# A state-space scan on one Trainium2 core: group loop unrolled, the next group's projection placed inside the scan, convolution read from PSUM, low weight parts on VectorE

## What is computed

```python
xbc = jax.nn.silu(causal_dwconv(xbc, conv_w, conv_b))      # xbc = hn @ w_in[...], 3072 columns, 4 taps
xs, Bm, Cm = split_cols(xbc, (SSD_D_INNER, SSD_BC, SSD_BC))
def ssd_chunk_step(S, inp):                                # 4 groups, 8 heads of 64, chunks of 64, state 128
    xdt, a, Bc, Cc = inp
    acum = jnp.cumsum(a, axis=1)
    seg = jnp.exp(-jnp.abs(acum[:, :, None] - acum[:, None, :]))
    cb = jnp.einsum('btgn,bsgn->btsg', Cc, Bc)
    y = jnp.einsum('btsgr,btsg,bsgrp->btgrp', seg, cb, xdt)
    y = y + jnp.einsum('btgn,bgrpn,btgr->btgrp', Cc, S, jnp.exp(acum))
    to_end = jnp.exp(acum[:, -1:] - acum)
    S = S * jnp.exp(acum[:, -1])[..., None, None] + jnp.einsum('bsgn,bsgr,bsgrp->bgrpn', Bc, to_end, xdt)
    return S, y
y = y + d_skip * xs_h
```

## Time and profile before

| | |
|---|---|
| runs | 2955.06, 2955.79 and 2959.34 us, median 2955.79 us |
| span of the profiled execution | 2945.8 us; its own time is not given apart, the runs lie 9.3 to 13.5 us above the span |
| busy over the span | PE 2838.9 us (96%), DVE 1991.9 (68%), ACT 1002.5 (34%), POOL 626.4 (21%) |
| `ssd_phase` | from 51.3 to 358.5 us, that is 307.2 us |

### The profile page before, as it was taken

The page is one execution under the profiler, slowest core; times in us unless marked ns, Lnnn a source line. Parts: engine busy times, 40 slices in busy tenths (PEclk is TensorE's granted clock), DMA queues, the critical chain, the costliest instruction groups (busy, mean ns, idle before and its releaser), DMA issues. The chain is left out here.

```text
span 2945.8 us, 43610 instructions
## 1 busy us (share of the span) xinstructions
PE 2838.9 (96%) x16114; PEld 2517.0 (85%) x16114; DVE 1991.9 (68%) x3329; ACT 1002.5 (34%) x1494; POOL 626.4 (21%) x444
## 2 busy tenths in 40 slices
PE   6999999999999999999999999999999999999998
PEld 5777677799787899999999999999999776788877
DVE  5878755334635468989967768777777655478843
ACT  3222244233333234344433333333334333322222
POOL 2333200000000037555654322222221000100000
PEclk9999999999999999999999999999999999999999
DMA  2111122211122237688999989999996211222232
GB/s 94 40 39 43 43 93 93 86 58 57 64 93 100 93 123 270 218 281 284 288 290 330 386 310 342 342 341 342 342 341 238 64 51 43 71 89 99 92 87 79
DMA packets 273015, 496.38 MB, mean 169 GB/s; under 512 B 121313, under 2 KB 178785, under 8 KB 272114
## 3 DMA queue, kind: packets, MB, share of 16 engines
q1 hardware_dynamic: 217586, 335.20, 34.4%
q0 software_dynamic: 36864, 134.23, 12.4%
q10 hardware_dynamic: 18432, 25.17, 2.3%
HBM read 442.10 MB, written 52.43 MB: 168 GB/s over the span
## 5 line engine op out<-in xcount | busy, mean ns | idle before, releaser
L283 PE MATMUL banks<-experts_third,weights_high 128*128 128x384 f32 x1024 | 346.1, 338 | 1.0 <-DVE experts_third L2024 1.0
L285 PE MATMUL banks<-experts_third,weights_low 128*128 128x384 f32 x1024 | 346.0, 338 | 0.0
L284 PE MATMUL banks<-experts_third,weights_high 128*128 128x384 f32 x1024 | 346.0, 338 | 0.0
L283 PE MATMUL banks<-hn_high,weights_high 128*128 128x264 f32 (+1 forms) x832 | 280.2, 337 | 7.8 <-PEq L515 2.9
L284 PE MATMUL banks<-hn_low,weights_high 128*128 128x264 f32 (+1 forms) x832 | 273.7, 329 | 0.0
L285 PE MATMUL banks<-hn_high,weights_low 128*128 128x264 f32 (+1 forms) x832 | 273.6, 329 | 0.0
L1838 POOL TENSOR_TENSOR weights_low<-weights_raw,weights_high 128x1024 fp32r<-128x1024 f32 x63 | 151.3, 2402 | 489.7 <-ACT weights_high L1740 489.5
L1797 ACT ACTIVATE weights_high<-weights_raw 128x1024 fp32r<-128x1024 f32 x128 | 135.9, 1062 | 346.7 <-PE banks L285 346.7
L283 PE MATMUL banks<-hb_high,weights_high 128*128 128x384 f32 x688 | 242.3, 352 | 9.5 <-POOL weights_low L1838 5.2
L284 PE MATMUL banks<-hb_low,weights_high 128*128 128x384 f32 x688 | 235.3, 342 | 0.0
L285 PE MATMUL banks<-hb_high,weights_low 128*128 128x384 f32 x688 | 235.2, 342 | 0.0
(11 more groups left out here) (565 smaller groups left out, 7125.3 us busy)
## 6 DMA issues: line engine op xcount, KB each, us to landing
weights_raw<-in_u SPq DMA_DIRECT2D x128, 512.0 KB, 6.9
weights_raw<-in_v SPq DMA_DIRECT2D x128, 512.0 KB, 5.8
early_experts<-experts_A ACTq DMA_DIRECT2D x128, 192.0 KB, 4.6
expert_weights<-shared SPq DMA_DIRECT2D x48, 512.0 KB, 7.4
shared<-expert_weights SPq DMA_DIRECT2D x128, 192.0 KB, 5.5
shared<-early_experts SPq DMA_DIRECT2D x128, 192.0 KB, 6.3
weights_raw<-in_w_up SPq DMA_DIRECT2D x44, 512.0 KB, 3.2
weights_raw<-in_w_xbc SPq DMA_DIRECT2D x24, 512.0 KB, 3.2
```

The costliest lines, as they stand in the source:

```text
L283: nc.tensor.matmul(to, w[0], x[0], start=start, stop=False)
L284: nc.tensor.matmul(to, w[0], x[1], start=False, stop=False)
L285: return nc.tensor.matmul(to, w[1], x[0], start=False, stop=stop)
```

## The change

`ssd_phase` is rewritten, and nothing else. Its parts:

1. The loops over groups are unrolled on every engine; semaphores are compared with constants.
2. The group's 6 tiles of the projection are moved: those of group 0 run first as before, those of group g + 1 are put between the steps of the scan of group g. The scan of the last group has `keep_running` in those places (14 matmuls in all); in the other groups there are none.
3. The product is convolved from PSUM. ScalarE's eviction (Copy) becomes the first tap and the bias (Identity with scale and bias, `first_tap`); the other three taps are three scalar_tensor_tensor of VectorE with the PSUM pair as one input, over all 528 positions, into a buffer that is shifted by an offset. The tensor_scalar goes.
4. The weight split: the high part moves from VectorE to ScalarE (`weight_high`), the low part from GpSimd to VectorE, behind each convolution (`split_low`).
5. The scaling by the skip weight moves from GpSimd to ScalarE. GpSimd keeps the 20 diagonals. Abs and Exp work on 4 blocks at once, one set a group.
6. PSUM: the projection has one pair of banks (0, 1; tile 1 of each group uses 4, 5) once the scan runs, where it had three; row part, turn-back, within and before have one bank each, where they had two. A tile's product waits for the last tile's convolution.

The core of the diff (the order on TensorE, and the two helpers that moved):

```diff
-                    for j in range(T):
-                        pe.wait_ge(low_done, g * T + j + 4)
...
-                        for b in SIDE.get(j, ()):
-                            row_part(b)
+                for m in range(T):
+                    tile_product(m)
+                    if m < 5:
+                        row_part(0, m)
+                for g in range(G):
+                    m, ahead = (g + 1) * T, g + 1 < G
+                    turn_x(g, 0)
+                    turn_x(g, 1)
+                    if ahead:
+                        tile_product(m)
+                    else:
+                        keep_running(k, 0, 3)
+                    if g:
+                        turn_back(g - 1, NB - 1)
+                    turn_x(g, 2)
+                    products_inside(g)
+                    turn_b(g)
+                    if ahead:
+                        tile_product(m + 1)
...
+                    turn_x(g, 3)
+                    turn_x(g, 4)
+                    if ahead:
+                        tile_product(m + 2)
...
+                    state_part(g, 0)
+                    state_part(g, 1)
+                    within(g, NB)
+                    within(g, 0)
+                    state_part(g, 2)
+                    before(g, 0)
+                    state_part(g, 3)
+                    if ahead:
+                        row_part(g + 1, 0)
+                        tile_product(m + 3)
+                    turn_back(g, NB)
+                    within(g, 1)
+                    before(g, 1)
+                    state_part(g, 4)
+                    state_part(g, 5)
+                    turn_back(g, 0)
+                    if ahead:
+                        row_part(g + 1, 1)
+                        tile_product(m + 4)
...
+                def weight_high(m):
...
+                    act.wait_ge(product, m - 1)
+                    nc.scalar.activation(high[:, m % 2, :], raw_w[:, m % 3, :], ACT.Copy).then_inc(high_done, 1)
...
+                def split_low(m):
+
+                    dve.wait_ge(high_done, m - 1)
+                    nc.vector.tensor_tensor(low_w[:, m % 2, :], raw_w[:, m % 3, :], high[:, m % 2, :].bitcast(F32), ALU.subtract
+                                            ).then_inc(low_done, 1)
+
+                def convolve(m):
+                    g, j = m // T, m % T
+                    dve.wait_ge(tap, m + 1)
+                    for s in (1, 2, 3):
+                        if m or s > 1:
+                            dve.wait_ge(convolved, 3 * m + s - 1)
+                        to = acc_at(m, s).rearrange(two, h=2)
+                        nc.vector.scalar_tensor_tensor(to, B[:, pair(m):pair(m) + 2, 0:264], conv[:, g, j, 3 - s:4 - s], to,
+                                                       ALU.mult, ALU.add).then_inc(convolved, 1)
+                    split_low(m + 2)
```

More of the change, by code:

```diff
@@ L989, in ssd_phase @@
         diag64 = k.const("diag64")
+        two = "p (h n) -> p h n"
+        full, meta = slice(0, P), slice(0, META)
         def heads(a, n=HD):
@@ new lines, in row_part @@
+                def row_part(g, b):
+                    r, n = rows_of(b)
+                    pe.wait_ge(diag, g * 5 + b + 1)
+                    if g or b:
+                        pe.wait_ge(diff, g * 5 + b)
+                    if g and b == 0:
+                        pe.wait_ge(m_ready, g * 5)
+                    nc.tensor.matmul(B[r, ROW_BANK, 0:H * n], k.const("same")[r, r] if b < NB else k.const("ones")[r, r],
+                                     X[r, b % 2, 0:H * n], start=True, stop=True).then_inc(row_done, 1)
@@ new lines, in before, with turn_back @@
+                def before(g, b):
+                    pe.wait_ge(state, g * 8 + 2 + 2 * b)
+                    for i in range(2):
+                        c = 1 + 2 * b + i
+                        last = nc.tensor.matmul(B[i * CH:i * CH + CH, BEFORE, :], bc[:, g % 2, 1, chunk_cols(c)],
+                                                S[:, (c - 1) % 4, :], start=True, stop=True)
+                    last.then_inc(y_done, 1)
+                def turn_back(g, b):
+                    r = full if b < NB else meta
+                    pe.wait_ge(y_tok, g * 5 + place(b))
+                    if g or b < NB:
+                        pe.wait_ge(y_out, g * 5 + place(b) - 1)
+                    for j in range(4):
+                        n = P if b < NB else META
+                        last = nc.tensor.transpose(B[:, BACK_BANK, j * n:(j + 1) * n], yt[r, 1 if b == NB else b % 2, j * P:(j + 1) * P],
+                                                   ident[r, r])
+                    last.then_inc(y_turned, 1)
@@ L1291 @@
+                add_skip(G - 1, NB - 1)
 SCORE_STEPS = 5 * (2 * PEER_HEADS + PEER_HEADS) + 25
```

553 lines of the change are left out of this document (303 added, 250 removed).

## The result

The changed kernel takes **2930.48 us** (median of 4 runs, 2928.13 to 2936.58) against 2955.43 (4 runs, 2950.99 to 2959.34): ratio 0.9925, 95% interval 0.9906 to 0.9943. It is faster by 0.75%, some 22 us by the ratio where 38 were forecast; the sign is as predicted. The median is 12 us over the forecast of 2918 and inside the range of 2903 to 2932, at its upper end. By the ratio, taken from the 2955.8 that the forecast started from, the time is 2933.6 us, just above that range. A third of the expected gain and more is missing, and the question is where it went.

A forecast was written before the change was run, and what follows sets the result against it. TensorE bounds a new group (58.7 us of work against VectorE's 51); 91.4 + 59.8 + 61.9 + 61.9 + 42.6 = 317.6 us against 358.5, less 3 for handovers, saves 38: 2918 us, range 2903 to 2932.

The forecast's parts named there:

- the mechanism of the overlap: In ssd_phase neither TensorE nor VectorE is full over a 77 us group, so projection and scan can be overlaid.
- The last scan: Group 3's scan, with no tiles left to overlay: 5.9 to the first turn, 34.3, and two bank waits, together 42.6 us.
- two waits of 1.2 for banks that aren't doubled any more: In the last scan, 1.2 us lost twice because banks are single; 2.4 us in the sum.
- The 5.9 to the first turn: Start of the last scan: 5.9 us until TensorE first turns x.
- TensorE's work per group: In each new group, tiles, turns, state products, within, before and row parts add up to 58.7 us.
- The waits (1.2 and 2.0 a group): Groups 1 and 2: TensorE waits 1.2 us for block 0's skip and 2.0 for the small row part's difference.
- The clock in overlapped groups: TensorE's granted clock was expected at 1.00 in the three overlapped groups; below 0.95 would show the forecast wrong.
- Rival 5: TensorE falls to 1.2 GHz in groups without dummies, up to 3022 us with all 18 tiles slow; chance 0.03.
- VectorE: 51 us of work in a new group, taps from PSUM at 0.74 us each, under TensorE's 58.7.
- GpSimd: Keeps only diagonals; taps with one SBUF input run free of it, low parts on VectorE can be held up.
- Rival 3, the lists interlock: TensorE and VectorE wait for each other on single banks, 1.5 us at four places a group; 2938 us, chance 0.08.
- The reading of the baseline: Runs of the kernel before were taken to lie about 10 us above the profiled span, left as it is.

The follow-up runs named there:

- the same kernel without the rotation: Changed kernel, but each group's six projection tiles stand ahead of its own scan again; 2997.32 us, ratio 1.0152 to the kernel before.
- The old order: Changed kernel with the last scan, from the third state on, in the previous kernel's step order, doubled banks, two more fillers: 2916.89 us; on the reordered kernel 2907.44.
- the reordered kernel: Changed kernel with VectorE's difference for row part 3 ahead of tile 5's low part, and meta rows turned back ahead of tile 3; 2917.76 us, ratio 0.9894.
- three kernels with more fillers: Filler matmuls added in group 0 and the last scan: to the changed kernel 2931.0 us, with doubled banks 2936.61, with doubled banks on the reordered kernel 2931.33.

## Why the prediction was right or wrong

- **Direction and the mechanism of the overlap: right.** Neither engine was full over a group, and laying the stages over one another paid: 67 us against the same kernel without the rotation.
- **The last scan: the step that failed.** The term was "what the scan of before has behind its convolutions, 38.2 less 3.9 = 34.3, and two waits of 1.2 for banks that aren't doubled any more: 42.6". It measured 54.3. The 5.9 to the first turn was right (289.98 to 295.95). The rest took durations from a scan whose order of steps, and whose clock, are others: the order rows showed where the tiles went, and I compared no others. The 11.7 us over the forecast are, by the stretches of the table:
  - 3.1 ahead of the first state (18.9, where the forecast had 13.8 and 2.0 more). VectorE has 3.7 us more of work there than in the scan of before (15.45 us busy against 11.73): the low part for the next phase, two skips, two differences and the tokens of the last block, less the first tap that ScalarE now makes. Low parts on GpSimd took 1.0 to 1.1 off this stretch (17.8 and 17.9 us). For the exponentials, which begin only behind the last difference, VectorE waits 0.15 us.
  - 6.0 in the middle. The parts within of the meta rows and of block 0 stand ahead of the third state, which costs about 6 at half clock and about 2 at full clock.
  - 3.9 to the end. A turn-back that waits for VectorE stands ahead of block 2, worth about 2; the rest goes with the clock (0.83).
  - 1.1 between the cut at 358.5 and the start of the next phase, less 2.4 for the single banks, which were charged for nothing: doubling them alone gave nothing.

  The old order, with its doubled banks, gives 9 to 10 us back: 45.0 and 43.8 us.
- **TensorE's work per group: 58.7, measured 61.05**, busy with no wait, 4% low, which is about 7 us over three groups. In group 2 of the reordered kernel, from start to start, 8 state products take 6.3 us where I charged 4.2, and 6 tiles 36.6 for 34.8; the other steps are together 1.2 below their terms. I read the row of 1.12 us at 195.97 as two state products, but "x2" is one, as every float32 matmul of the scan shows as two. Only two that stand side by side take that time together (1.13 us for x4, at 334.32 in the changed kernel). The waits (1.2 and 2.0 a group) were right in place and size, since reordering the lists took away 2.95.
- **The clock in overlapped groups: wrong for one of three.** Forecast 1.00, measured 0.97, 1.00 and 0.90. The 0.97 is a slow start behind the 4.0 us wait for silu (two turns of x in 1.97 us, 1.03 at full clock). Rival 5 put a fall down to waits and missing dummies; the costly one in group 3 (4.8 of the 6.3 us) came in gapless work, only the 1.5 us in the turn of x behind a wait.
- **VectorE: right.** 50 us busy against 51, taps 0.766 long against 0.71. Three take 2.38 us, a pitch of 0.81 where I took 0.74. By the Trainium skill, page "VectorE: DVE Perf Modes", section on the TRN2 errata, PSUM costs more than SBUF to read, and the estimate from it (4.7 us for 72 taps) has the size of this surcharge (72 times 0.07 is 5.0); but a sum out of a bank is no dearer than a decay out of SBUF (0.687 and 0.703), so these rows don't show that it is the cause.
- **GpSimd: right.** Taps stayed at 0.766 with GpSimd nearly idle and at 0.767 with its low parts, the decays rose from 0.703 to 0.819. By the Trainium skill, page "SBUF — State Buffer", section "Who interferes with whom", an instruction with one SBUF input doesn't meet GpSimd and one with two does: the traces agree.
- **Rival 3, the lists interlock, comes nearest to what happened**, at 0.08, with 2938 for it; but its sign, over 5 us of waits for VectorE a group, did not show (3.3 a group). The interlock was in the last scan, where no tile covers it, and not at four places of each group.
- **The reading of the baseline: wrong.** I wrote that the runs lie about 10 us above the span. They don't: in all runs measured later time and span differ by 1.8 to 2.9 us, and the profiled execution of the kernel before (span 2945.8) was one of its quick ones. So the phase, 15.3 us shorter between the two profiles, is compared with a lucky one; the medians differ by 20 to 25. Where in the program the usual run of before is slower was not looked at.
- **That the time is only 12 us off is in part luck.** The profiled span is 2934.8 us where 2907.8 was forecast, 27.0 more: 23.7 in the phase and the rest behind it. Of this the 10 us put between span and time, where 1.8 belong, take 8 back, and 6 lie between the profiled execution (2936.58) and the median.

## What to carry to other kernels

When a change writes a list anew, compare the order of all its steps, not only of the ones that moved: a duration of the old schedule holds only for the old order. Overlapping stages covers a poor order wherever there is other work, so look for what it costs in the last turn of the loop, which has no next one to cover it, and keep an order of its own there. And before buying back a low granted clock with filler work, see whether the slow steps stand in anybody's way; putting the step that others wait for first (with the doubled banks that the old order had) gave 13 us, where fillers shortened the last scan by 4 and the whole by nothing.

## What the hardware showed that I had not expected

- The granted clock fell to half in the middle of gapless work, where TensorE did the scan's short steps (64 columns and 512 columns by turns). In the changed kernel's group 3 this cost 4.8 us. Of 14 profiles with rotated groups six had one or more (the change twice in group 3, others in group 1 or 2, one in both), and kernels with the same list up to there had it in group 3, in group 2 or not at all. It came in five of the nine profiles with the change's order in the groups and in none of the four reordered kernels without added fillers, which is too few to name the order as the cause. What decides it stays open.
- The three kernels with more fillers spent 2593.6, 2596.8 and 2596.4 us behind the phase; the kernel before 2586.2 and the eleven other profiles with the rotation 2583.8 to 2590.5. What fillers won inside the phase was lost behind it. The cause was not shown: the granted clock behind the phase is 0.99 in all of them, and the kernel without the rotation spent 2593.4 us there without added fillers.
- ScalarE's eviction out of PSUM takes 0.79 us with scale and bias for each partition (Identity, 24 times), where the plain copy of the same 528 columns took 0.61.
